# Row sums spread through DRAM, and half of a modulation vector summed on GpSimd, in a hybrid decoder block

## The chip, the cores and the metric

One core of one Trainium2 chip. The metric is the device time of one execution in microseconds (us), the median over runs; lower is better. Engines: TensorE (PE, with its weight loads as PEld), VectorE (DVE), ScalarE (ACT), GpSimd (POOL) and SyncE (SP), which here only issues DMAs.

## What is computed

One layer of a decoder trunk on x of 1024 tokens by 1024 channels, float32. A vector c gives shifts, scales and gates:

```python
c_act = jax.nn.silu(c)
mod = c_act @ w_mod[l] + b_mod[l]                      # 6 x 1024
h = _modulate(_rmsnorm(x, norm1_gain[l]), sh1, sc1)
x = x + g1 * _hybrid_mixer(h, ...)                     # attention and output projection
h = _modulate(_rmsnorm(x, norm2_gain[l]), sh2, sc2)
x = x + g2 * _swiglu(h, w_gate[l], w_up[l], w_down[l])
sh_f, sc_f = jnp.split(c_act @ w_mod_final + b_mod_final, 2, axis=-1)
return _modulate(_rmsnorm(x, final_gain), sh_f, sc_f)
```

The mixer has eight stick-breaking heads and eight sparse heads of 64. For a sparse head each query takes its 256 best keys by an indexer; then

```python
logits = q @ k_sel * scale - slopes * dist             # masked where not valid
p = jax.nn.softmax(logits, axis=-1)
out = p @ v_sel
```

Both groups are RMS-normalised, joined and multiplied by w_o (1024 x 1024).

## The kernel before, in words

The program is written out by hand, one instruction stream per engine, in two blocks with a barrier between them: phase 0 and 1 (modulation, norm, input projection, index selection) and the attention; then `phase4` (output projection and first residual) and `phase5` (FFN, final norm).

**Attention.** `attention` (L993) walks over 128 rows: 16 heads (8 stick-breaking, then 8 sparse), each with its eight 128-query blocks from the widest (i = 7, 1024 keys) to the narrowest (i = 0). Step r does the logits of row r + 2 on TensorE, row r on VectorE, and for the sparse half the exponential of row r - 1 on ScalarE (L1218), with its row sums into `sm`. Four rows are a group (`gr`, 32 in all; the upper group of a head has rows 7 to 4, the lower rows 3 to 0). A group's probabilities are transposed five steps later, block by block (L1469), copied from PSUM to `aT` by ScalarE (L1242) or VectorE (L1350), and multiplied with the values into the one PSUM bank `o` (L1487). The transposes' places are chosen by `attention_plan`: the bank `ps_at`, or the free half of a logits slot `ps_z`; for each it also says which earlier block must have been copied out.

A sparse group is divided by its row sums at the end. The sums stand one per partition (query), but `o` has the queries along its free dimension, so they have to be spread: VectorE takes the reciprocals of a group's 4 x 128 sums (L1354, step 4 d + 5 of the sparse half for group d); TensorE multiplies each column, broadcast, with an identity into a bank (L1494, step 4 d + 8; eight passes recorded for four matmuls); ScalarE copies 64 lanes of it to `spr` (L1249); VectorE multiplies `o` with it into `of` (L1365, step 4 d + 9), and that frees `o` for TensorE. SP loads `w_mod` tiles all through the attention, GpSimd sums them (L1278 product, L1282 sum).

**Output projection.** `phase4` (L1508) makes 16 half rows y(n) of 128 x 512. TensorE computes the stick-breaking part `y_sb` (L1678, three ahead) and the sparse part `y_d` (L1694), 12 matmuls each. ScalarE scales the first (L1627), VectorE adds the second (L1780, `y_full`), gates it (L1792) and adds it to x (L1795). Behind x of steps 0 to 7 VectorE does four of 32 steps of the final modulation vector: `fa` = `fa` + c_act[t] * w_mod_final tile (L1756 first of a quarter, L1759 the others). SP loads the tiles (L1593, four buffers) and stores `fa` after every quarter of eight steps (L1592, L1600); the next quarter waits for that store. ScalarE squares finished rows of x (L1617); after the fourth, GpSimd computes 1/rms of the first four rows (L1646, L1648, "early rstd"), VectorE scales them ahead of y step 8 (`early_xhat`, L2055), and TensorE transposes them between the later y steps (L2049); ScalarE modulates each transposed tile (L2015). SP stores every finished row of x (L2007) between its loads.

Of the kernel before, what the change touches and what calls it, by code (L numbers as in the profile page):

```python
# [25 lines left out]
P = 128  # L26
# [966 lines left out]
def attention(nc, k, g, A, scr, p1, base):  # L993
# [9 lines left out]
    def extra(r, end):  # L1003
        v = [("v", 2 * (r // (2 * NT)) + x) for x in range(2)] if values_at(r) else []
        return v, [("s", gr) for gr in range(SBG, 2 * SBG) if end.get(gr, -99) == r]
# [63 lines left out]
    sd = k.sem("rsum_spread_done")  # L1069
    sc = k.sem("rsum_spread_copied")  # L1070
# [28 lines left out]

    def spread(r):  # L1100
        return [gr for gr in end if gr >= SBG and end[gr] == r]
# [93 lines left out]
    def scalar(act):  # L1195
# [12 lines left out]
        for r in range(STEPS):  # L1208
# [4 lines left out]
            if SBR < r <= NR:  # L1213
# [5 lines left out]
                               accum_out=sm[:, c:c + 1]).then_inc(ex, 1)  # L1219
            if values_at(r):  # L1220
# [22 lines left out]
            for gr in spread(r):  # L1243
                d = gr - SBG
                lanes = slice(HD * (gr // 2 % 2), HD * (gr // 2 % 2) + HD)
                act.wait_ge(sd, d + 1)
                if d >= 4:
                    act.wait_ge(od, gr - 3)
                act.activation(spr[lanes, upper(gr)], place(("s", gr))[lanes], ACT.Copy).then_inc(sc, 1)  # L1249
# [60 lines left out]
    def vector(dve):  # L1310
        dve.wait_ge(cset, 1 + NPB)
        for r in range(STEPS):
# [42 lines left out]
            for gr in ended(r, 1):  # L1355
# [7 lines left out]
                else:  # L1363
                    dve.wait_ge(sc, gr - SBG + 1)
# [14 lines left out]
    def tensor(pe):  # L1379
        def await_freed(e):  # L1380
# [5 lines left out]
            elif kind == "s":  # L1386
                pe.wait_ge(sc, n - SBG + 1)
            else:
                pe.wait_ge(*copied(n))
# [59 lines left out]
        for r in range(STEPS):  # L1449
# [39 lines left out]
            for gr in spread(r):  # L1489
                d = gr - SBG  # L1490
                await_freed(follows["s", gr])
                pe.wait_ge(rc, d + 1)
                for b in range(4):
                    last = pe.matmul(place(("s", gr))[:, P * b:P * b + P],  # L1494
                                     rs[:, 4 * d + b:4 * d + b + 1].to_broadcast([P, P]), g.ident[:],
                                     start=True, stop=True)
                last.then_inc(sd, 1)
# [10 lines left out]
def phase4(nc, ctx, k, g, A, modf, then):  # L1508
# [14 lines left out]
    NFW = 4  # L1523
    fw = nc.alloc_sbuf_tensor_at("wmod_final", [P, NFW, HALF], F32, offset=g.top - 8 * 1024)
    ps_a, ps_b, ps_m = g.ps[:, 0:NSB], g.ps[:, NSB:NSB + ND4], g.ps[:, NSB + ND4]
# [26 lines left out]
    NF, FY = 4 * KD, 8  # L1552
# [24 lines left out]
    def sync(sp):  # L1577
# [16 lines left out]

        for n in range(NY):
            for f in final_steps(n):
                load_final(f)
# [1254 lines left out]
```

## Time and profile before

| what | us |
|---|---|
| median of 3 runs (1447.98 to 1451.27) | 1448.45 |
| the profiled execution | 1446.68 |
| its span in the profile | 1445.0 |
| TensorE busy | 1341.7 (93%) |
| VectorE busy | 1023.3 (71%) |
| GpSimd busy | 727.8 (50%) |
| ScalarE busy | 684.6 (47%) |

The span runs from the first to the last recorded instruction of the profiled execution; times within it are from its start. "Busy" leaves out waits, semaphore and DMA-issuing instructions. The chain of waits follows back from the last instruction what released each step. The sparse half of the attention lies at about 508 to 674 us, the output projection at 676 to 790 us.

### The profile page before, as it was taken

The numbers are of one execution on the slowest core, as the hardware profiler recorded it, in microseconds if no ns is written. First come the engines' busy times: TensorE is split into PE (matmuls) and PEld (weight loads), VectorE is DVE, ScalarE is ACT, GpSimd is POOL, SyncE is SP. The second block draws the span as 40 slices with busy tenths as digits, with TensorE's granted clock in tenths as the row PEclk, the third lists the DMA queues.
The fourth block names the chain that finished last, engine by engine and source line by source line (L and its number), as shares of the span: only waits on it lengthen the run. The fifth ranks groups of instructions, "written<-read, shape, count | busy, mean of one in ns | idle before, by whom it ended". The sixth has DMA issues, their size and how long they took to land.

```text
span 1445.0 us, 18548 instructions
## 1 busy us (share of the span) xinstructions
PE 1341.7 (93%) x6181; PEld 1071.6 (74%) x6181; DVE 1023.3 (71%) x1468; ACT 684.6 (47%) x1157; POOL 727.8 (50%) x628
## 2 busy tenths in 40 slices
PE   2899999997899999989998899999999999999997
PEld 2668888785566666657876778888888888887886
DVE  4678699987877655554775986666666666378787
ACT  5456677736676655554125633223323334354332
POOL 3135444556677866652002165555555556578552
PEclk9899899998999999998999999999999999999999
DMA  9521234457534343312753244444444435989432
GB/s 326 178 62 30 88 126 135 144 162 203 131 76 114 88 125 116 89 43 84 272 172 114 88 152 155 167 168 167 168 158 146 146 141 197 362 296 327 150 109 117
DMA packets 123562, 220.20 MB, mean 152 GB/s; under 512 B 9386, under 2 KB 52500, under 8 KB 123220
## 3 DMA queue, kind: packets, MB, share of 16 engines
q1 hardware_dynamic: 123476, 219.12, 45.7%
q8 instruction: 46, 0.75, 0.2%
q14 instruction: 40, 0.33, 0.1%
HBM read 160.90 MB, written 57.93 MB: 151 GB/s over the span
## 4 chain that ended last, share of the span: by engine, by line
PE 41%; DVE 7%; issue 2%; DMA 1%; ACT 1%; POOL 0%; DVEq 0%; POOLq 0%; ACTq 0%
PE ps_out L2339 25%; PE ps_out L2365 12%; PE ps_out L1694 1%; DVE mod_acc_final L1759 1%; PE ps_out L1678 1%; DMA scr_mod_final<-mod_acc_final 1%; DVE y_full L1780 1%; DVE wgu_lo L2446 0%; PE ps_out L1702 0%; ACT square_junk L2257 0%; DVE x L2601 0%; DVE y_gated L1792 0%; DVE down_part L2599 0%; DVE h_sum_t L2413 0%; DVE h_t_full L2413 0%
## 5 line engine op out<-in xcount | busy, mean ns | idle before, releaser
L2036 POOL TENSOR_TENSOR wgu_lo<-wgu_raw,wgu_hi 128x512 fp32r<-128x512 f32 x66 | 97.4, 1483 | 127.6 <-ACT wgu_hi L2028 127.6
L2273 POOL TENSOR_TENSOR dn_lo<-dn_raw,dn_hi 128x512 fp32r<-128x512 f32 x77 | 126.9, 1665 | 67.1 <-ACT dn_hi L2179 67.0
L2028 ACT ACTIVATE wgu_hi<-wgu_sum 128x512 fp32r<-128x512 f32 x88 | 55.2, 632 | 199.7 <-DVE wgu_sum L2429 80.0
L2339 PE MATMUL ps_out<-h_b_t_hi,wgu_hi 128*128 128x512 f32 x352 | 138.1, 392 | 6.6 <-DVE h_b_t_lo L2417 2.6
L483 POOL TENSOR_TENSOR win_lo<-win_raw,win_hi 128x256 fp32r<-128x256 f32 (+1 forms) x84 | 66.7, 824 | 141.0 <-ACT win_hi L473 115.7
L2339 PE MATMUL ps_out<-h_b_t_hi,wgu_lo 128*128 128x512 f32 x352 | 137.7, 391 | 0.0
L2339 PE MATMUL ps_out<-h_b_t_lo,wgu_hi 128*128 128x512 f32 x352 | 137.5, 391 | 0.0
L2179 ACT ACTIVATE dn_hi<-dn_raw 128x1024 fp32r<-128x1024 f32 x77 | 81.2, 1062 | 114.4 <-PE ps_out L2365 55.7
L2365 PE MATMUL ps_out<-dn_hi 128*128 128x512 f32 x308 | 120.2, 390 | 0.0
L2365 PE MATMUL ps_out<-dn_hi,dn_lo 128*128 128x512 f32 x308 | 119.8, 389 | 0.0
L2365 PE MATMUL ps_out<-dn_lo,dn_hi 128*128 128x512 f32 x308 | 119.8, 389 | 0.0
L2497 DVE TENSOR_TENSOR dn_lo<-dn_raw,dn_hi 128x512 fp32r<-128x512 f32 x77 | 84.7, 1132 | 44.6 <-ACT dn_hi L2179 44.6
L1292 POOL TENSOR_TENSOR a_rows<-beta,stick_left 128x1024 f32<-128x1024 f32 (+3 forms) x64 | 83.7, 1314 | 49.0 <-DVE stick_left L1319 28.6
L839 DVE TENSOR_SCALAR_CACHE_REDUCE cmp_junk<-score,thr 128x768 uint8<-128x768 f32 (+3 forms) x96 | 103.8, 1131 | 1.3 <-DVE thr L863 0.2
L2036 POOL TENSOR_TENSOR wgu_lo<-wgu_sum,wgu_hi 128x512 fp32r<-128x512 f32 x40 | 60.7, 1519 | 76.3 <-ACT wgu_hi L2028 76.3
L1319 DVE TENSOR_TENSOR_SCAN stick_left<-ps_z,scan_zero 128x1024 f32<-128x1024 f32 (+3 forms) x64 | 85.5, 1345 | 12.2 <-ACT ps_z L1205 8.2
L107 PE MATMUL ps_proj<-hTh,win_hi 128*128 128x512 f32 (+1 forms) x288 | 90.1, 394 | 2.6 <-ACT proj_full L593 1.6
L107 PE MATMUL ps_proj<-hTl,win_hi 128*128 128x512 f32 (+1 forms) x288 | 89.7, 393 | 0.0
L107 PE MATMUL ps_proj<-hTh,win_lo 128*128 128x512 f32 (+1 forms) x288 | 89.4, 392 | 0.0
L631 ACT ACTIVATE cmp_junk<-score,thr 128x384 int8<-128x384 f32 (+2 forms) x93 | 66.0, 711 | 36.3 <-DVE thr L863 36.2
L2339 PEld LDWEIGHTS ps_out<-h_b_t_hi,wgu_hi 128*128 128x128 f32 x352 | 66.5, 189 | 21.4 <-issue 5.2
L1487 PE MATMUL ps_o<-aT,vd 128*128 128x512 f32 (+1 forms) x192 | 73.8, 493 | 4.1 <-DVE o_full L1365 2.9
(356 smaller groups left out, 3648.9 us busy)
## 6 DMA issues: line engine op xcount, KB each, us to landing
scr_act_sums<-act_sums SPq DMA_DIRECT2D x11, 1792.0 KB, 6.7
dn_raw<-scr_act_sums SPq DMA_DIRECT2D x77, 256.0 KB, 5.3
wmod_c<-in_w_mod_dram SPq DMA_DIRECT2D x48, 256.0 KB, 2.9
wgu_raw<-in_w_gate_dram SPq DMA_DIRECT2D x11, 1024.0 KB, 5.3
wgu_raw<-in_w_up_dram SPq DMA_DIRECT2D x11, 1024.0 KB, 5.4
wd_sums<-in_w_down_dram SPq DMA_DIRECT2D x11, 1024.0 KB, 4.8
scr_wd_sums<-wd_sums SPq DMA_DIRECT2D x11, 1024.0 KB, 4.1
dn_raw<-scr_wd_sums SPq DMA_DIRECT2D x44, 256.0 KB, 7.0
```

The source lines that it names most:

```text
L107: last = pe.matmul(ps[:, s], w[:, t, :], x[:, t, s], start=(t == 0 and w is wh and x is xh), stop=(t == KD - 1 and w is wl))
L483: last = pool.tensor_tensor(low[:, t:t + 2, 0:w], raw[:, n % 2, t:t + 2, 0:w], high[:, t:t + 2, 0:w].bitcast(F32), ALU.subtract)
L839: last = dve.tensor_scalar(junk[:, w], g.score[:, w], at(i - 2), None, op, ALU.add, accum_out=cnt[:, i - 2:i - 1])
L1292: pool.tensor_tensor(a[gr % 2][:, rows[r][1] % 4, 0:w], bt[:, r % NB, 0:w], pb[:, r % NPB, SEQ - w + 1:SEQ + 1], ALU.mult).then_inc(mul, 1)
L1319: dve.tensor_tensor_scan(pb[:, r % NPB, SEQ - w:SEQ][:, ::-1], z[:, r % NZ, 0:w][:, ::-1], zero[:].to_broadcast([P, w]), 1.0, ALU.mult, AL ...
L1487: pe.matmul(o[:, s], v, aT[:, n % NA, s], start=(b == 0), stop=(b == 4 * upper(gr) + 3), skip_group_check=True).then_inc(vd, 1)
L2036: pool.tensor_tensor(sl[slot(m, x)][:], src, sh[slot(m, x)][:].bitcast(F32), ALU.subtract).then_inc(wlp, 1)
L2179: act.activation(bh[q % NSLOT][:], braw[entry(q)][:], ACT.Copy).then_inc(dhi, 1)
L2273: pool.tensor_tensor(bl[q % NSLOT][:, 1], braw[entry(q)][:, 1], bh[q % NSLOT][:, 1].bitcast(F32), ALU.subtract).then_inc(dlw, 1)
L2339: last = pe.matmul(bank(m, b), a[s][:, t], h[x][t // 2][:, t % 2], start=(fresh and t == 0 and a is sh and h is hh), stop=(t == 3 and a is ...
L2365: last = pe.matmul(ps[:, y], a[s][:, 0, P * b:P * b + P], w[s][:, 1], start=(fresh and q % NPR == 0 and a is bh and w is bh), stop=(q % NP ...
L2497: dve.tensor_tensor(bl[q % NSLOT][:, 0], braw[entry(q)][:, 0], bh[q % NSLOT][:, 0].bitcast(F32), ALU.subtract).then_inc(dla, 1)
```

## The change

Part one: a sparse group's reciprocals are no longer spread by TensorE and ScalarE. ScalarE stores the 512 floats to a DRAM row (step 4 d + 6), waits for that store at step 4 d + 7, and loads the row back, broadcast to the 64 lanes of `spr`. VectorE waits for the load where it waited for the copy. The planner has no place to find for the spread any more.

Part two: of the final modulation vector VectorE sums the first two quarters, GpSimd the last two, each in a tile of its own (`fa`, `fb`) with two load buffers (`fw`, `fx`) instead of four. GpSimd does them after `rstd_col` and ahead of the early rstd. SP issues for each f first the GpSimd load, then the VectorE load.

```diff
@@ attention
-        return v, [("s", gr) for gr in range(SBG, 2 * SBG) if end.get(gr, -99) == r]
+        return v, []
@@ attention, scalar, behind the exponential of step r
+            d = (r - SBR - 6) // 4
+            if r >= SBR + 6 and r % 4 == 2 and d < SBG:
+                act.wait_ge(rc, d + 1)
+                act.dma_start(rsum[d].rearrange("(b p) -> p b", p=P), rs[:, 4 * d:4 * d + 4],
+                              allow_slow_non_contiguous=True).then_inc(rso, 16)
@@ attention, scalar, behind the copies to aT
-            for gr in spread(r):
-                d = gr - SBG
-                lanes = slice(HD * (gr // 2 % 2), HD * (gr // 2 % 2) + HD)
-                act.wait_ge(sd, d + 1)
+            d = (r - SBR - 7) // 4
+            if r >= SBR + 7 and r % 4 == 3 and d < SBG:
+                lanes = slice(HD * (d // 2 % 2), HD * (d // 2 % 2) + HD)
+                act.wait_ge(rso, 16 * (d + 1))
                 if d >= 4:
-                    act.wait_ge(od, gr - 3)
-                act.activation(spr[lanes, upper(gr)], place(("s", gr))[lanes], ACT.Copy).then_inc(sc, 1)
+                    act.wait_ge(od, SBG + d - 3)
+                act.dma_start(spr[lanes, upper(d)], rsum[d:d + 1, :].partition_broadcast(HD)).then_inc(rsl[d % 2], 16)
@@ attention, vector
-                    dve.wait_ge(sc, gr - SBG + 1)
+                    dve.wait_ge(rsl[gr % 2], 16 * ((gr - SBG) // 2 + 1))
                     dve.tensor_tensor(of[lanes, G], o[lanes], spr[lanes, G], ALU.mult).then_inc(od, 1)
@@ attention, tensor
-            for gr in spread(r):
-                d = gr - SBG
-                await_freed(follows["s", gr])
-                pe.wait_ge(rc, d + 1)
-                for b in range(4):
-                    last = pe.matmul(place(("s", gr))[:, P * b:P * b + P],
-                                     rs[:, 4 * d + b:4 * d + b + 1].to_broadcast([P, P]), g.ident[:],
-                                     start=True, stop=True)
-                last.then_inc(sd, 1)
@@ phase4
-    NFW = 4
+    fb = nc.alloc_sbuf_tensor_at("mod_acc_final_pool", [P, HALF], F32, offset=g.top - 14 * 1024)
+    NFW = 2
     fw = nc.alloc_sbuf_tensor_at("wmod_final", [P, NFW, HALF], F32, offset=g.top - 8 * 1024)
+    fx = nc.alloc_sbuf_tensor_at("wmod_final_pool", [P, NFW, HALF], F32, offset=g.top - 4 * 1024)
-    NF, FY = 4 * KD, 8
+    NF, FY = 2 * KD, 8
@@ phase4, sync
+        def load_final_pool(f):
+            c, t = f // KD, f % KD
+            if f >= NFW:
+                sp.wait_ge(fpa, f - NFW + 1)
+            if f >= KD and t == NFW - 1:
+                sp.dma_start(modf[:, half(2 + c - 1)], fb[:]).then_inc(fpo, 16)
+            sp.dma_start(fx[:, f % NFW], A["w_mod_final"][P * t:P * t + P, half(2 + c)]).then_inc(fxl[f % NFW], 16)
+
         for n in range(NY):
             for f in final_steps(n):
+                load_final_pool(f)
                 load_final(f)
             if n == FY:
                 sp.wait_ge(fmd, NF)
-                sp.dma_start(modf[:, half(3)], fa[:]).then_inc(fmo, 16)
+                sp.dma_start(modf[:, half(1)], fa[:]).then_inc(fmo, 16)
+                sp.wait_ge(fpa, NF)
+                sp.dma_start(modf[:, half(3)], fb[:]).then_inc(fpo, 16)
@@ phase4, gpsimd, behind rstd_col and ahead of the early rstd
+        for f in range(NF):
+            c, t = f // KD, f % KD
+            pool.wait_ge(fxl[f % NFW], 16 * (f // NFW + 1))
+            by = g.csil[:, t:t + 1].to_broadcast([P, HALF])
+            if t == 0:
+                if c:
+                    pool.wait_ge(fpo, 16 * c)
+                pool.tensor_tensor(fb[:], fx[:, f % NFW], by, ALU.mult).then_inc(fpa, 1)
+            else:
+                pool.tensor_tensor(fx[:, f % NFW], fx[:, f % NFW], by, ALU.mult).then_inc(fpr, 1)
+                pool.wait_ge(fpa, f)
+                pool.wait_ge(fpr, f - c)
+                pool.tensor_tensor(fb[:], fb[:], fx[:, f % NFW], ALU.add).then_inc(fpa, 1)
         pool.wait_ge(s2, 4)
@@ phase5, scalar and sync: wherever all of fmo (fmd) is awaited
-            act.wait_ge(p4.fmo, 64)
+            act.wait_ge(p4.fmo, 32)
+            act.wait_ge(p4.fpo, 32)
```

## Rows read from the trace of the kernel before

**Rows 1.** The page, busy time: us, share of the span, instructions.

```profile
PE 1341.7 (93%) x6181; PEld 1071.6 (74%) x6181; DVE 1023.3 (71%) x1468; ACT 684.6 (47%) x1157; POOL 727.8 (50%) x628
```

**Rows 2.** Stretch of one sparse head: length, busy by engine, clock, DMA.

```profile
598.80:619.00 20.20, 18.86 (x102) 13.57 (x101) 10.62 (x29) 10.97 (x26) 15.08 (x14) 1.00 0.39 110
```

**Rows 3.** Timeline, TensorE, projection: start, us, what [idle before, and releaser].

```profile
752.90 0.66 PE L2049 MATMUL ps_out<-ident,x 128*128 128x128 f32 x4 [0.72 <-DVE x L2055]
...
759.56 1.09 PE L2049 MATMUL ps_out<-ident,x 128*128 128x128 f32 x4 [3.24 <-ACT h_sum_b L2015]
```

**Rows 4.** The tile scr_mod_final, all its DMAs: time to landing.

```profile
DMA to landing us min/median/max: 2.4/4.6/5.0
```

**Rows 5.** Timelines of VectorE, GpSimd and SP in the projection.

```profile
750.12 2.73 DVE L2055 TENSOR_SCALAR x<-x,rstd 128x1024 f32<-128x1024 f32 x4
...
748.60 1.01 POOL L1648 TENSOR_TENSOR rstd<-rstd,nhalf 128x4 f32<-128x4 f32 x1
...
706.79 0.33 SPq L2007 DMA_DIRECT2D scr_x<-x  x1
```

**Rows 6.** Timeline, TensorE, around both spreads of one head.

```profile
599.46 1.05 PE L1494 MATMUL ps_at<-ident,prob_rsum 128*128 128x128 f32 x8
601.20 0.66 PE L1469 MATMUL ps_at<-ident,a_rows 128*128 128x128 f32 x4 [0.68 <-ACT rsum_spread L1249]
...
607.00 1.05 PE L1494 MATMUL ps_at<-ident,prob_rsum 128*128 128x128 f32 x8
607.89 1.04 PE L1469 MATMUL ps_z<-ident,a_rows 128*128 128x128 f32 x8
```

**Rows 7.** Timeline, VectorE: widest row of the first two sparse heads.

```profile
498.46 1.28 DVE L1334 CUSTOM_DVE_ANT_0 a_rows<-ps_z,score,nslope 128x1024 f32<-128x1024 f32 x1 [3.13 <-PE ps_at L1469]
...
516.22 1.28 DVE L1334 CUSTOM_DVE_ANT_0 a_rows<-ps_z,score,nslope 128x1024 f32<-128x1024 f32 x1 [3.11 <-PE ps_at L1469]
```

**Rows 8.** Timelines of VectorE and ScalarE in that head of rows 6.

```profile
597.55 1.28 DVE L1334 CUSTOM_DVE_ANT_0 a_rows<-ps_z,score,nslope 128x1024 f32<-128x1024 f32 x1 [3.11 <-PE ps_at L1469]
...
598.96 1.14 DVE L1334 CUSTOM_DVE_ANT_0 a_rows<-ps_z,score,nslope 128x896 f32<-128x896 f32 x1
...
602.70 1.03 ACT L1218 ACTIVATE a_rows<-a_rows,neg_max 128x896 f32<-128x896 f32 x1
...
603.84 1.00 DVE L1334 CUSTOM_DVE_ANT_0 a_rows<-ps_z,score,nslope 128x768 f32<-128x768 f32 x1
...
605.82 0.81 ACT L1218 ACTIVATE a_rows<-a_rows,neg_max 128x640 f32<-128x640 f32 x1
...
609.66 0.65 DVE L1365 TENSOR_TENSOR o_full<-ps_o,rsum_spread 64x512 f32<-64x512 f32 x1
```

**Rows 9.** DMA: issues with count, KB each, median us to landing; queue's packets.

```profile
q1 hardware_dynamic: 123476, 219.12, 45.7%
...
wmod_c<-in_w_mod_dram SPq DMA_DIRECT2D x48, 256.0 KB, 2.9
...
wmod_final<-in_w_mod_final_dram SPq DMA_DIRECT2D x32, 256.0 KB, 4.0
...
scr_x<-x SPq DMA_DIRECT2D x8, 512.0 KB, 2.8
...
wukv_raw<-in_w_uk_dram SPq DMA_DIRECT2D x1, 64.0 KB, 2.0
```

**Rows 10.** Stretch at the projection's first steps; last numbers: DMA share, GB/s.

```profile
696.00:699.00 3.00, 3.00 (x14) 2.46 (x14) 0.15 (x1) 0.00 (x0) 0.00 (x0) 1.00 1.03 390
```

**Rows 11.** GpSimd's product and sum in the attention: ns min/median/max, first, last start.

```profile
L1278 POOL TENSOR_TENSOR mod_prod_c<-wmod_c,csil x42: 1032/1041/3022, 362.6 to 649.1; 128x512 f32<-128x512 f32 x42
...
L1282 POOL TENSOR_TENSOR mod_acc_late<-mod_acc_late,mod_prod_c x28: 1261/1276/1291, 525.8 to 650.2; 128x512 f32<-128x512 f32 x28
```

**Rows 12.** Timeline, GpSimd and VectorE, where both read two SBUF tiles.

```profile
838.07 1.62 POOL L2265 TENSOR_TENSOR wd_sums<-wd_sums 128x512 f32<-128x512 f32 x1
...
846.94 1.77 DVE L2486 TENSOR_TENSOR act_sums<-act_sums 128x512 f32<-128x512 f32 x1
```

More of the change, by code:

```diff
@@ L990, in attention_plan, with attention @@
     return rows, units, of_step, end, done_by, bank, follows, row_follows
-def attention(nc, k, g, A, scr, p1, base):
+def attention(nc, k, g, A, scr, rsum, p1, base):
     NZ, LEAD, VSTEP = 3, 5, 3
@@ L1068, in attention @@
     rc = k.sem("d_rsum_ready")
-    sd = k.sem("rsum_spread_done")
-    sc = k.sem("rsum_spread_copied")
+    rso = k.sem("rsum_stored")
+    rsl = k.sems("rsum_spread_loaded", 2)
     oll = k.sem("oT_lo_last_ready")
@@ L1098, in ended @@
         return [gr for gr in end if end[gr] + steps == r]
-    def spread(r):
-        return [gr for gr in end if gr >= SBG and end[gr] == r]
     def paired(r, steps):
@@ L1385, in await_freed @@
                 pe.wait_ge(v_rdy, n + 1)
-            elif kind == "s":
-                pe.wait_ge(sc, n - SBG + 1)
             else:
@@ L1551, in phase4 @@
     fmo = k.sem("mod_final_stored")
-    NF, FY = 4 * KD, 8
+    fxl = k.sems("wmod_final_pool_loaded", NFW)
+    fpr = k.sem("mod_final_pool_product")
+    fpa = k.sem("mod_final_pool_added")
+    fpo = k.sem("mod_final_pool_stored")
+    NF, FY = 2 * KD, 8
     STEP_T = {(1, 10): 0, (0, 10): 1, (1, 11): 2, (0, 11): 3, (1, 12): 4, (0, 12): 5, (1, 13): 6, (0, 13): 7}
@@ L1802, in phase4 @@
     p.yam, p.yfr, p.ysc, p.x1r, p.s2, p.rs2, p.fmd, p.fmo, p.ybm = yam, yfr, ysc, x1r, s2, rs2, fmd, fmo, ybm
+    p.fpa, p.fpo = fpa, fpo
     p.NY, p.NF = NY, NF
@@ L2139, in sync @@
                 sp.wait_ge(u2n, 4)
-                sp.wait_ge(p4.fmo, 64)
+                sp.wait_ge(p4.fmo, 32)
+                sp.wait_ge(p4.fpo, 32)
                 sp.dma_start(mfin[:], modf.rearrange("p (c n) -> p c n", c=4)).then_inc(mfl, 16)
@@ L2181, in scalar @@
         act.wait_ge(p4.fmd, p4.NF)
+        act.wait_ge(p4.fpa, p4.NF)
         copy_p1(0)
@@ L2700, in emit @@
         scr = nc.dram_tensor("scr_qkv", [16, 2, P, SEQ], F32, kind="Internal").ap()
+        rsum = nc.dram_tensor("scr_rsum", [2 * NH, HALF], F32, kind="Internal").ap()
         modf = nc.dram_tensor("scr_mod_final", [P, 2 * D], F32, kind="Internal").ap()
@@ L2759, in emit @@
                 assert base + 68 * 1024 <= nc.sbuf_top
-                pa = attention(nc, k, g, A, scr, p1, base)
+                pa = attention(nc, k, g, A, scr, rsum, p1, base)
                 with nc.Block() as block:
```

## The prediction

> **What bounds the kernel now.** I read the page's busy shares first, then the chain of waits, then the two stretches that the diff touches: the sparse half of the attention (508 to 674 us) and the output projection (676 to 790 us). TensorE is busy 93% of the span [rows 1]. In the sparse half one head takes 20.2 us; TensorE works 18.9 of them, VectorE and ScalarE 11, GpSimd up to 15 [rows 2]: TensorE goes through its instructions nearly without a gap. So it does in the projection, up to the first transposes of the normed rows at 752.90, where it waits 0.72 us, and the next at 759.56, where it waits 3.24 us [rows 3]. VectorE is the late one there. The chain of waits has it three times at the store of a finished quarter of the final modulation vector, which lands in 4.6 us at the median [rows 4], and the scaling of x that the transposes read (L2055) starts only at 750.12 [rows 5].
>
> **Part one: the spread leaves TensorE.** Each of the 16 groups loses eight TensorE passes (L1494) and one ScalarE copy (L1249). For a lower group the passes begin at 607.00 and what follows begins at 607.89: 0.89 us. For an upper group it is 599.46 to 601.20, 1.74 us, since the next transposes also wait for ScalarE's copy out of the same bank, 0.68 us [rows 6]. That wait is there in seven of the eight heads. That makes 1.74 + 0.89 = 2.63 us a head. The trace has a check on it: the first sparse head runs while no spread is due yet, and from its widest row to the next head's it takes 516.22 - 498.46 = 17.8 us [rows 7] instead of 20.2 [rows 2], 2.4 less. I take the 2.4, which has the waits in it that come in the spread's place: 7 x 2.4 = 16.8 us, and the last head 2 x 0.89 = 1.8: gross 18.6 us. The planner now places the transposes of steps 5 and 6 otherwise: a block then waits for ScalarE's copy of one step before, which comes earlier too, without the spread's copy in front of it. I take 0 for that.
>
> What is added is on ScalarE's queue: at step 2 or 6 of a head's eight a store of 512 single floats, at step 3 or 7 a wait for its landing, then the broadcast load. Behind the wait stand the exponentials of the next rows, and TensorE's transposes wait for the fourth of them. Take the lower group in the head at 597 us, with rows named by their key block. VectorE ends row 7 at 598.83 and row 6 at 600.1; the spread's copy no longer holds ScalarE, so row 6's exponential (1.03) runs from 600.1, or from 600.5 in every second head, where a square stands between: the store goes out at 601.1 or 601.5. VectorE's row 5 ends at 603.1 (604.84 moved 1.74 up), its exponential near 604.05, being a little longer than row 4's 0.81. Then the load's issue, 0.35 as on SP [rows 5], and row 4 with the gap behind it, 0.9: done at 605.3. TensorE now wants it at 607.89 - 2.63 = 605.26 [rows 6, 8]. So a store that has landed costs nothing. The cover is 605.26 - 0.9 - 0.35 - 601.1 (or 601.5) = 2.9 (or 2.5) us of landing, and each us beyond costs 1 us a head.
>
> How long does such a store take? The trace has none. A 512 KB store lands in 2.8 us, a 64 KB load in 2.0, a 256 KB load in 2.9 [rows 9]. 512 KB at the 390 GB/s of a full stretch [rows 10] are 1.3 us, so 1.5 are fixed: the lower end. For the upper end let each float cost what a mean packet costs: 45.7% of 16 engines' 1445 us over 123476 packets is 86 ns, and 32 of them per engine 2.7 us, on top of the 2.4 us of the shortest store in the projection: 5.1 [rows 4, 9]. I take 2.7 us, nearest to the 512 KB store: a piece of 4 bytes should cost less than a packet with data. The loss is then 0 or 0.2 us a head, with some row-4 jitter 1.5 us in all. At 1.5 us there is none, at 5.1 it is 8 x 2.4 = 19.2 us. The upper groups have more cover: behind their store and one more exponential ScalarE waits for TensorE's transposes anyway (its copy of 613.7), and then come exponentials that nobody wants before the next head. The load's 128 KB should lie between the 64 and the 256 KB, 2.4 us, and land 5.5 us after the store's issue, at 606.8 or so; VectorE's product wants it at 609.66 - 2.63 = 607.0 [rows 8]. That is even, and behind it on VectorE stand only rows of which TensorE wants none for 1 us.
>
> Each group also has two more waits for a DMA, and a released wait lets a little pass before the next instruction starts: 16 times some 0.07 us, 1.1 us, my allowance and not a row. Part one: -18.6 + 1.5 + 1.1 = -16 us.
>
> The Trainium skill, DMA: Bandwidth & Descriptors, "Rules for kernel authors", says that a strided last dimension becomes one descriptor per element, and its section "Anatomy of one DMA" gives about 2 us of fixed cost per transfer, most of it the receipt of the write. It speaks against this edit. By its 2 us the store would be within the cover; no row here shows the cost of one such element.
>
> **Part two: half of the final vector to GpSimd.** VectorE loses 16 steps and two of three waits for a store. But what holds TensorE is the start of the scaling at 750.12, and that also waits for GpSimd's early rstd, ready at 749.61 [rows 5]. In the new code GpSimd comes to this rstd only after its 16 steps. So the question is when the sixteenth ends.
>
> A step on GpSimd is a product, 1.04 us, and a sum, 1.28, alone [rows 11]. It will not be alone. Where VectorE and GpSimd both read two SBUF tiles, a VectorE instruction of 0.69 us takes 1.77 and GpSimd's sum takes 1.62, one pair each 1.7 us [rows 12]; VectorE has four such in every y step. I take 3.3 us a step. A load takes 2.9 to 4.0 us [rows 9]; I take 3.3, for one or two are in flight and not five. A buffer's load is issued when its last reader is done, so with two buffers two steps cost one landing and one step, 6.6 us. The first loads sit behind the x rows, which fill the DMA engines until 699 [rows 10]; the second step ends at about 701. Seven pairs more: 46.2 us. SP's queue adds to it: the third and fourth GpSimd load stand behind loads that wait for VectorE's first steps, and the fifth behind the first x1 store (706.79) [rows 5], 2 us; the ninth step waits for the store of a half (4.6 instead of 3.3), 1.3 us. Sum: 750.5. Then rstd, 1.4 us, and a gap: the scaling starts at 752.1 instead of 750.12. The transposes and the chain behind them (y steps 8 and 9 on VectorE, square, ScalarE's modulation) move with it: +2.0 us. VectorE itself keeps up: 0.8 + 4 x 1.6 = 7.2 us in a step at worst beside TensorE's 5.45, which puts y step 7 near 746. SP's wait for the sixteenth step holds back only x1 stores that aren't ready, ScalarE's new waits are long over.
>
> The ends: if the two engines did not slow each other, a step costs 2.4 and a pair 5.7, the sixteenth ends 6.3 us earlier, and both waits of TensorE (0.72 and 3.24) [rows 3] go: -4 us. If every load takes 4.0, seven pairs cost 5 us more, less what the waits on SP then hide: +6 us.
>
> **Sum.** -16 + 2 = -14 us. The profiled execution took 1446.68 us, 1.68 more than its span; the median of the runs is 1448.45. So 1432.7 there, and 1434.5 at the median.
>
> **Rivals.**
> (a) GpSimd's instructions keep their 1.04 and 1.28 us. For it: VectorE will idle in part. Against: the long instructions of [rows 12]. Part two is then -4 instead of +2: -20, 1428.5.
> (b) GpSimd is far behind, by loads of 4.0 us or longer blocking: part two +6, sum -10, 1438.5. The Trainium skill, SBUF — State Buffer, "SBUF: two separate sides", calls the shared port an exclusive lock, the loser fully blocked. By that a pair would cost 0.69 + 1.28 = 1.97 us; the trace's 1.7 has them overlap a little, so this case stays the weaker one.
> (c) The store lands at 4.0 to 4.5 us: 1.3 to 1.8 us a head, 10 to 14 us and not 1.5; total -5 to -1: 1445. For it: 512 pieces beside SP's weight loads on the same DMA engines. Against: nothing queues in front of it.
> (d) Slower than before: ScalarE's wait for the store decides. Its place is step 3 of each sparse head, its price 8 us per us of landing, and what the sum leaves is eaten at 2.7 + 15.5 / 8 = 4.6 us. At 5.9 us: 8 x 3.2 = 25.6 and not 1.5, so +10: 1458.5.
> (e) The spread's passes only filled time in which TensorE would wait anyway for another engine's rows: part one gives nothing, the kernel is at +2 to +4, 1451. Against it: the first head's 17.8 us [rows 7], and that no other engine has more than 15 of 20.2 us [rows 2].
>
> **How the numbers follow.** Main case 0.52, (a) 0.12, (b) 0.14, (c) 0.14, (d) and (e) 0.08 together. The range 1427 to 1446 holds the first three and the better half of (c). A measurement of this kernel can't tell a change under 0.3%, 4.3 us, from none: faster 0.84, same 0.08, slower 0.08.
>
> **What would show it.** A sparse head of about 18.0 us, with no L1494 and no wait of L1469 for a spread. The store's landing near 2.7 us. TensorE waiting at L1469 for ScalarE's a_rows by less than 0.5 us a head. In the projection GpSimd busy from 697 to 750.5 (all 16 us earlier by then), its instructions 1.2 to 1.7 us long; L2055 right behind rstd L1648; the wait of the first transposes (L2049) grown from 0.72 to near 3 us. I am wrong if the store's landing is over 3.5 us, if heads stay at 20 us, or if GpSimd's last step ends before VectorE's.

## The result, and the profile after

| | before | after |
|---|---|---|
| median of 4 runs each, us | 1449.10 (1447.98 to 1451.27) | 1518.32 (1513.26 to 1526.00) |
| ratio, 95% interval | | 1.0493 (1.0470 to 1.0517) |
| profiled execution / its span, us | 1446.68 / 1445.0 | 1515.03 / 1513.3 |
| mean granted clock of TensorE | 0.977 | 0.952 |
| widest row of the first to that of the last sparse head, us | 144.05 | 192.20 |

The kernel is 4.9% slower where a gain of 14 us was forecast. Span and busy time of the changed kernel, from its page:

```profile
PE 1350.9 (89%) x6053; PEld 1076.4 (71%) x6053; DVE 1030.3 (68%) x1452; ACT 678.6 (45%) x1141; POOL 766.7 (51%) x658
```

TensorE has 128 instructions fewer than in [rows 1] and still is busy for 9 us more. Both have one cause, and one sparse head shows it. Stretches of the changed kernel, in the columns of [rows 2]: the whole head, and 4 us pieces of it.

```profile
603.72:631.78 28.06, 19.51 (x86) 14.02 (x85) 10.96 (x26) 10.88 (x25) 10.96 (x10) 0.88 0.44 70
```
```profile
604.00:608.00 4.00, 4.00 (x24) 3.00 (x22) 3.43 (x8) 2.44 (x5) 3.42 (x4) 1.00 0.41 111
608.00:612.00 4.00, 3.56 (x15) 1.80 (x13) 3.37 (x9) 1.46 (x3) 3.55 (x4) 1.00 0.54 114
612.00:616.00 4.00, 0.00 (x0) 0.00 (x0) 0.40 (x2) 0.00 (x0) 0.11 (x1) 1.00 0.02 6
616.00:620.00 4.00, 2.42 (x12) 2.46 (x13) 0.45 (x1) 2.98 (x8) 0.00 (x0) 0.54 0.26 33
620.00:624.00 4.00, 4.00 (x16) 3.44 (x16) 2.47 (x8) 2.12 (x5) 1.54 (x2) 0.61 1.12 162
```

From 612 to 616 everything stands, the DMA engines included (share 0.02). What it stands for is in ScalarE's timeline, and in TensorE's behind it: the store goes out at 607.08, the load that waits for it at 616.01.

```profile
607.08 0.37 ACTq L1220 DMA_DIRECT2D scr_rsum<-prob_rsum  x1
...
616.01 0.45 ACTq L1251 DMA_DIRECT2D rsum_spread<-scr_rsum  x1
616.51 0.83 ACT L1215 ACTIVATE a_rows<-a_rows,neg_max 128x640 f32<-128x640 f32 x1 [6.08 <-DMA scr_rsum<-prob_rsum]
...
629.98 0.63 ACT L1256 ACTIVATE o_dT_hi<-o_full 128x512 fp32r<-128x512 f32 x1 [3.66 <-DMA scr_rsum<-prob_rsum]
```
```profile
617.58 1.09 PE L1469 MATMUL ps_at<-ident,a_rows 128*128 128x128 f32 x4 [5.93 <-ACT a_rows L1215]
...
631.32 0.33 PE L1469 MATMUL ps_at<-ident,a_rows 128*128 128x128 f32 x1 [2.54 <-ACT aT L1244]
```

The exponential of row 4 (640 keys) starts 6.08 us late and TensorE's transposes 5.93 us late; the upper group's store holds ScalarE once more for 3.66 us, and through ScalarE's copy TensorE for 2.54 us. After the first stop the granted clock is 0.54 and 0.61 in the next two pieces, so nearly at the lower of its two levels (1.2 of 2.4 GHz), where the kernel before stays at 1.00 through such a head [rows 2]. The head's 28.06 us are 19.51 busy and 8.55 idle.

The same from the widest row of the first sparse head to the start of the projection block, before and changed:

```profile
498.46:676.50 178.04, 160.69 (x842) 114.16 (x840) 94.78 (x221) 94.60 (x218) 98.14 (x84) 1.00 0.27 80
```
```profile
498.77:736.60 237.83, 167.72 (x714) 117.07 (x712) 96.12 (x221) 88.52 (x202) 98.52 (x84) 0.88 0.42 69
```

Of the 59.8 us that the stretch is longer, TensorE idles for 52.8 (70.1 against 17.4) and works for 7.0 (167.7 against 160.7), although its 128 passes of the spread are gone.

The waits of the whole stretch 490 to 760 (engine, tile and line; releaser; us in total, times, longest), and how long the stores and the loads took (us to landing, minimum, median, maximum):

```profile
ACT a_rows L1215 <- DMA scr_rsum<-prob_rsum: 61.9, 12, 6.7
...
PE ps_at L1469 <- ACT a_rows L1215: 42.4, 8, 6.6
POOL mod_prod_c L1280 <- DMA wmod_c<-in_w_mod_dram: 42.2, 12, 7.9
...
PE ps_at L1469 <- ACT aT L1244: 16.6, 8, 4.1
```
```profile
L1220 ACTq DMA_DIRECT2D scr_rsum<-prob_rsum x16: 361/367/423, 508.7 to 719.6; - x16
DMA to landing us min/median/max: 7.7/9.0/9.7
```
```profile
L1251 ACTq DMA_DIRECT2D rsum_spread<-scr_rsum x16: 452/452/503, 518.4 to 727.4; - x16
DMA to landing us min/median/max: 3.2/4.1/7.6
```
```profile
wmod_c<-in_w_mod_dram SPq DMA_DIRECT2D x48, 256.0 KB, 7.0
```

A store of 2 KB takes 9.0 us, nearly twice the upper end that I had given it (5.1), and SP's loads of the attention's modulation weights land in 7.0 us instead of 2.9 [rows 9].

In the projection the first transposes of the normed rows wait 7.45 us where they waited 0.72 [rows 3]. VectorE, GpSimd and TensorE of the changed kernel there:

```profile
815.12 1.82 DVE L1780 SCALAR_TENSOR_TENSOR mod_acc_final<-wmod_final,csil,mod_acc_final 128x512 f32<-128x512 f32 x1 [2.82 <-DMA wmod_final<-in_w_mod_final_dram]
818.13 2.74 DVE L2078 TENSOR_SCALAR x<-x,rstd 128x1024 f32<-128x1024 f32 x4 [1.19 <-POOL rstd L1669]
```
```profile
815.13 1.26 POOL L1665 TENSOR_TENSOR mod_acc_final_pool<-mod_acc_final_pool,wmod_final_pool 128x512 f32<-128x512 f32 x1
816.48 0.52 POOL L1667 TENSOR_SCALAR rstd<-ss 128x4 f32<-128x4 f32 x1
817.08 1.02 POOL L1669 TENSOR_TENSOR rstd<-rstd,nhalf 128x4 f32<-128x4 f32 x1
```
```profile
820.92 1.12 PE L2072 MATMUL ps_out<-ident,x 128*128 128x128 f32 x4 [7.45 <-DVE x L2078]
```

The projection block begins at 736.6 and not at 676.5, so 60.1 of the 68.3 us of span are lost before it. Its last y_full starts at 855.01 instead of 787.32, 67.7 us later: another 7.6 us in the block, and next to nothing behind it. (The expectations of part1, part2 and both_16b work with 61.4 and 6.3 us, from a start read as 737.9.)

### The profile page after: what moved, and what is told of

It reads as the page before. It is cut to its first block, busy times and chain, and to the rows that moved or that the text cites. A ratio compares the mean times of both kernels' runs of the same rounds, so it can differ in the third digit from the quotient of the medians.

```text
span 1513.3 us, 18305 instructions
## 1 busy us (share of the span) xinstructions
PE 1350.9 (89%) x6053; PEld 1076.4 (71%) x6053; DVE 1030.3 (68%) x1452; ACT 678.6 (45%) x1141; POOL 766.7 (51%) x658
## 4 chain that ended last, share of the span: by engine, by line
PE 40%; DVE 5%; issue 2%; POOL 2%; DMA 1%; ACT 1%; SPq 0%; DVEq 0%; POOLq 0%; ACTq 0%
PE ps_out L2364 25%; PE ps_out L2390 12%; PE ps_out L1715 1%; DMA wmod_final_pool<-in_w_mod_final_dram 1%; PE ps_out L1699 1%; POOL mod_acc_final_pool L1665 1%; POOL wmod_final_pool L1662 0%; PE ps_out L1723 0%; DVE x L1816 0%; DVE y_full L1801 0%; ACT square_junk L2282 0%; DVE y_gated L1813 0%; DVE x L2626 0%; DVE down_part L2624 0%; DVE wgu_lo L2471 0%
## 5 line engine op out<-in xcount | busy, mean ns | idle before, releaser
L1469 PE MATMUL ps_at<-ident,a_rows 128*128 128x128 f32 x282 | 54.3, 309 | 65.4 <-ACT a_rows L1215 42.4
L1469 PEld LDWEIGHTS ps_at<-ident,a_rows 128*128 128x128 f32 x282 | 39.6, 159 | 88.7 <-issue 61.7
L1215 ACT ACTIVATE a_rows<-a_rows,neg_max 128x1024 f32<-128x1024 f32 (+3 forms) x64 | 49.3, 771 | 86.4 <-DMA scr_rsum<-prob_rsum 61.9
```

Of the source, the lines that this page charges most:

```text
L1469: last = pe.transpose(place(("u", n))[:, P * q:P * q + P], a[gr % 2][:, q, P * b:P * b + P], g.ident[:])
```

## The experiments

Twelve kernels, in four groups; each group ran on one chip with its own runs of the kernel before, and each ratio is against those.

| kernel | time, us | ratio to before, 95% | landing of the store, us |
|---|---|---|---|
| part1 | 1529.56 | 1.0539 (1.0507 to 1.0572) | 9.9 |
| part2 | 1451.58 | 1.0012 (0.9999 to 1.0025) | none |
| p1_sp | 1519.42 | 1.0480 (1.0456 to 1.0504) | 9.5 |
| p1_nowait | 1477.40 | 1.0204 (1.0163 to 1.0244) | 9.6 |
| p1_nostore | 1427.97 | 0.9852 (0.9831 to 0.9872) | none |
| probe | 1447.85 | 1.0003 (0.9988 to 1.0019) | three shapes |
| p1_16b | 1426.79 | 0.9860 (0.9835 to 0.9885) | 2.9 |
| both_16b | 1432.53 | 0.9899 (0.9881 to 0.9916) | 2.7 |
| both_early | 1436.01 | 0.9916 (0.9898 to 0.9935) | 3.0 |
| probe2 | 1448.19 (one run) | | three shapes |
| both_idle | 1424.82 | 0.9826 (0.9799 to 0.9853) | 3.0 |
| both_light | 1430.07 | 0.9870 (0.9847 to 0.9893) | 3.0 |

### Which part, and who waits

**part1** has only the hunks of the attention, **part2** only those of the output projection.

> The first part alone: sparse sums through DRAM, the final modulation vector left whole on VectorE as before. Theory (the store decides): ScalarE stands before its load until the store has landed, which in the changed kernel took 9.0 us, so sparse heads take 27 to 31 us here too, and the kernel 1512 us (1518.3 less the 6.3 that the projection block lost). Rival (the two parts hurt each other, or the loss sits in GpSimd's part): under 1470 us.

> The second part alone: half of the final modulation vector on GpSimd, the sparse sums spread on TensorE as before. Theory: the projection block is longer by the 6.3 us that it was in the changed kernel, because GpSimd's sixteenth step ends only then and the scaling of x waits for it: 1449.1 + 6.3 = 1455.4 us. Rival (that loss came over from the slow start, from transfers or clock of the attention block): 1449 to 1451 us, the sixteenth step 74 us after the block's start instead of 78.5.

The first part alone is 5.4% slower, the second 0.1%. So all of the large loss is the first part's. part1 is 18 us above the 1512 that I expected and 11 us slower than both parts together; its store took 9.9 us and not 9.0, but it ran on another chip, so I read nothing into that. For the second part the first theory's 1455.4 was too much: 1449.19 became 1451.58, +2.4 us. Its trace still has TensorE waiting 5.1 us for the scaling of x, which starts 77.9 us after the block's start where it was 73.6 before.

**p1_sp** moves wait and load to SyncE:

```
             # ScalarE, step 3 or 7 of a head
-            act.wait_ge(rso, 16 * (d + 1))
...
-            act.dma_start(spr[lanes, upper(d)], rsum[d:d + 1, :].partition_broadcast(HD)).then_inc(rsl[d % 2], 16)
             # SyncE, ahead of its next load of modulation weights
+            sp.wait_ge(rso[d % 4], 16 * (d // 4 + 1))
...
+            sp.dma_start(spr[lanes, upper(d)], rsum[d:d + 1, :].partition_broadcast(HD)).then_inc(rsl[d % 2], 16)
```

> The first part alone, with the wait for the store and the load issued by SyncE instead of ScalarE, ahead of the next weight load of its queue. Theory (what costs is that ScalarE stands in that wait with exponentials and copies queued behind it): the store still takes about 9 us, ScalarE's 61.9 us of waiting are gone, and the kernel comes to 1440 to 1465 us, the rest being VectorE's wait for the later load. Rival (the store itself slows the other transfers and the clock, whoever waits): it stays at 1495 to 1515 us.

ScalarE's waits were gone, and the time stayed, 1519.42: my theory fell, and the rival's 1495 to 1515 was a little low. Where the wait went is in the answer for VectorE's product (who it waited for, and who waited for it; us, times):

```profile
  DMA rsum_spread<-scr_rsum: 83.3, 11
  PE ps_o L1499: 2.3, 4
who waited for it (us, times):
  PE ps_o L1499: 68.0, 11
```

Store and load one after the other are 9.5 + 5.3 = 14.8 us at the medians, longer than a half head of 9 to 10 us. TensorE needs ps_o back within that, whichever engine stands in the wait. So this run moved the wait and did not take it away; it doesn't decide between theory and rival.

**p1_nowait** keeps stores and loads, but the load reads rows of the final modulation weights and needs no store. **p1_nostore** leaves out the store too.

```
-            act.wait_ge(rso, 16 * (d + 1))
...
-            act.dma_start(spr[lanes, upper(d)], rsum[d:d + 1, :].partition_broadcast(HD)).then_inc(rsl[d % 2], 16)
+            act.dma_start(spr[lanes, upper(d)], A["w_mod_final"][d:d + 1, 0:HALF].partition_broadcast(HD)).then_inc(rsl[d % 2], 16)
```

> The first part alone, but the load reads rows of the final modulation weights instead of the stored sums, so nothing waits for the store; the same stores and loads are made, and the values that scale the sparse heads are wrong. Theory (the wait decides): granted clock of the sparse heads back at 1.00, heads at 17.8 to 20.2 us, kernel 1430 to 1440 us, though the store still takes 9 us. Rival (interference of the 512 small pieces with the other transfers): modc weight loads still land late, kernel over 1480 us.

> The first part alone without any store of the sums; the load reads rows of the final modulation weights, so the values that scale the sparse heads are wrong. Against the kernel that keeps the stores but waits for none (1477 us) it shows what the stores cost by being in the queues. Theory (512 pieces hold up the load behind them and SyncE's weight loads): the load lands in 2 to 4 us, heads at 17.8 to 20.2 us, 1430 to 1436 us. Rival (16 spread loads of 128 KB are themselves too much for queues and buffers): modulation weights still land 5 us or later and the kernel stays over 1450 us.

DMA issues of the two, 490 to 760 us (KB each, median us to landing), first p1_nowait, then p1_nostore:

```profile
wmod_c<-in_w_mod_dram SPq DMA_DIRECT2D x37, 256.0 KB, 8.0
...
rsum_spread<-in_w_mod_final_dram ACTq DMA_DIRECT2D x16, 128.0 KB, 8.5
...
scr_rsum<-prob_rsum ACTq DMA_DIRECT2D x16, 2.0 KB, 9.6
```
```profile
wmod_c<-in_w_mod_dram SPq DMA_DIRECT2D x37, 256.0 KB, 2.9
...
rsum_spread<-in_w_mod_final_dram ACTq DMA_DIRECT2D x16, 128.0 KB, 3.0
```

Neither theory was right about p1_nowait: it lay between them, at 1477, and its heads behind the first take 21.5 to 26.1 us. Taking the wait away gives back 1529.6 - 1477.4 = 52 us, taking the store away another 1477.4 - 1428.0 = 49 us (across two chips; by the ratios 51). In p1_nowait nothing waits for the store. But a load issued behind it takes 8.5 us instead of 3.0, and SyncE's loads, on another queue, 8.0 instead of 2.9: while the slow store is under way, other transfers are late. Which of them costs time is in the waits of p1_nowait:

```profile
DVE o_full L1367 <- DMA rsum_spread<-in_w_mod_final_dram: 40.4, 13, 6.7
...
PE ps_o L1487 <- DVE o_full L1367: 33.4, 13, 5.7
```

VectorE's product waits for the load behind the store, and TensorE for the product. SyncE's late loads hold GpSimd (66.9 us, 20 times), and no wait of TensorE in the attention leads back to them. In part1 and the changed kernel the load is issued only when the store has landed, so the 52 and the 49 us are the same slow store met in two ways, not two costs of the changed kernel side by side.

### What makes the store slow

> The kernel before, with ScalarE issuing a store of the four columns of reciprocals once per half head, which nothing waits for until the block's end, in three shapes in turn: 512 pieces of 4 bytes side by side in DRAM (six times), 128 pieces of 16 bytes (five), 512 pieces of 4 bytes each 64 bytes from the next (five). Theory (a store costs by its pieces): 9 to 10 us, 3.5 to 4 us, 9 to 10 us. Rival (it costs because neighbouring 4-byte writes hit the same 64 bytes of DRAM): the spaced one lands in under 5 us. Time 1449 plus what the transfers behind the stores lose: up to 16 x 1.5 us, to 1473 us, if they are delayed as in the changed kernel, 1449 to 1452 if the modulation loads have that much slack.

> The kernel before with unwaited stores, as in the first probe, in three further shapes: 512 pieces of 4 bytes each 8 bytes from the next (8 share 64 bytes of DRAM), each 16 bytes from the next (4 share them), and one column alone, 128 pieces of 4 bytes side by side (16 share them). Theory (writes into the same 64 bytes go one after the other, about 0.5 us each: 16 of them 8.9 us, at most 4 of them 2.3 to 2.6): 4.5 us, 2.6 us, and 8 to 9 us for the one column although it has a quarter of the pieces. Rival (each 4-byte piece that has neighbours costs by itself, 512 of them 8.9 us): 8.9, 8.9 or 2.6, and 3 to 4 us for the one column.

Both probes are the kernel before plus one store per half head that nothing waits for, in shapes taken in turn. In the first the time is that of the kernel before: its 9 us stores were one in three and nobody was waiting. The edit of the first (the second changes the target's pattern, and for the one column the source):

```
+                act.wait_ge(rc, d + 1)
+                src = rs[:, 4 * d:4 * d + 4]
+                x = d % 3
+                dst = (lambda: prb[0][d].rearrange("(b p) -> p b", p=P),
+                       lambda: prb[1][d].rearrange("(p b) -> p b", p=P),
+                       lambda: prb[2][d].rearrange("(b p) x -> p b x", p=P)[:, :, 0])[x]()
+                act.dma_start(dst, src, allow_slow_non_contiguous=True).then_inc(prd[x], 16)
```

The answers for three of the shapes, one tile each: prb_4b and prb_4b_lines of the first probe, prb_4b_one_column of the second.

```profile
L1229 ACTq DMA_DIRECT2D prb_4b<-prob_rsum x6: 366/367/423, 506.6 to 662.6; - x6
...
DMA to landing us min/median/max: 8.2/8.9/11.8
```
```profile
L1229 ACTq DMA_DIRECT2D prb_4b_lines<-prob_rsum x5: 366/366/417, 526.7 to 653.5; - x5
...
DMA to landing us min/median/max: 1.9/2.6/3.9
```
```profile
L1229 ACTq DMA_DIRECT2D prb_4b_one_column<-prob_rsum x5: 338/338/353, 529.4 to 655.6; - x5
...
DMA to landing us min/median/max: 7.4/7.9/9.2
```

All six shapes:

| shape | pieces that share 64 bytes of DRAM | landing, us: median (lowest to highest), count |
|---|---|---|
| 512 x 4 B, side by side | 16 | 8.9 (8.2 to 11.8), 6 |
| 128 x 4 B, side by side (one column) | 16 | 7.9 (7.4 to 9.2), 5 |
| 512 x 4 B, every 8 B | 8 | 5.3 (3.1 to 7.8), 6 |
| 512 x 4 B, every 16 B | 4 | 3.0 (2.5 to 4.7), 5 |
| 128 x 16 B, side by side | 4 | 2.3 (1.4 to 9.5), 5 |
| 512 x 4 B, every 64 B | 1 | 2.6 (1.9 to 3.9), 5 |

The wide range of the 16 byte shape goes with what was ahead of it: its five landings are 1.4, 1.4, 2.3, 7.0 and 9.5 us, and the last two are those of the stores issued at 546.9 and 608.0, while the 4 byte store before them (539.7 and 600.9, landing after 8.2 and 11.8 us) was still under way. Before the other three it had landed.

My theory of the first probe fell: the same 512 pieces of 4 bytes land in 2.6 us when each has 64 bytes to itself. The number of pieces hardly matters, for a quarter of them, side by side, still takes 7.9 us. The time goes with how close together the pieces lie: counted by blocks of 64 bytes, one piece in a block lands in 2.6 us, and up to sixteen add about 0.4 us each ((5.3 - 2.6) / 7, (8.9 - 2.6) / 15), those with four a little less. That they are done one after the other in a block is a reading that fits the six shapes; the trace shows landings only. The 64 is the spacing that I tried, and these six shapes don't fix the size of the block. With blocks of 16 bytes the counts are 4, 4, 2, 1, 1, 1 in the table's order, with blocks of 512 they are 128, 128, 64, 32, 32, 8, and both put the shapes in about the same order. A block of 8 bytes doesn't fit, for with it a piece every 8 bytes would be as fast as one every 64.

The Trainium skill, DMA: Bandwidth & Descriptors, "Specifications", says that below 512 bytes the DMA engine reads, modifies and writes. It gives no price. All six shapes have pieces below that size, so this alone doesn't tell them apart; the runs show three of them at 2.3 to 3.0 us, and slow ones only where 4 byte pieces lie side by side or every 8 bytes.

### The repair

**p1_16b** is part1 with the four values of a partition stored side by side, 16 bytes at a time; VectorE reads the spread row with a stride to undo that.

```
-            act.dma_start(rsum[d].rearrange("(b p) -> p b", p=P), rs[:, 4 * d:4 * d + 4],
+            act.dma_start(rsum[d].rearrange("(p b) -> p b", p=P), rs[:, 4 * d:4 * d + 4],
...
-            dve.tensor_tensor(of[lanes, G], o[lanes], spr[lanes, G], ALU.mult).then_inc(od, 1)
+            dve.tensor_tensor(of[lanes, G].rearrange("q (b p) -> q b p", p=P),
+                              o[lanes].rearrange("q (b p) -> q b p", p=P),
+                              spr[lanes, G].rearrange("q (p b) -> q b p", p=P), ALU.mult).then_inc(od, 1)
```

> The first part alone, its store in 128 pieces of 16 bytes (the four sums of a partition side by side) and VectorE's product reading the spread row with a stride of 16 bytes to undo that order; the output is the reference's. Theory (the cost is the number of pieces, each at about 7.5 us / 512): store 3.5 to 4 us, ScalarE's wait under 1.5 us a half head, kernel 1440 to 1450 us. Rival (the landing of a small DRAM store is what it is): store 7 us or more and kernel over 1480 us.

1426.79 us, better than both theories: 103 us less than part1 (across two chips; by the ratios 98) by the order in which the values lie in DRAM. Its store's landing, and one of its heads:

```profile
L1220 ACTq DMA_DIRECT2D scr_rsum<-prob_rsum x16: 321/327/368, 509.1 to 646.8; - x16
DMA to landing us min/median/max: 1.4/2.9/6.4
```
```profile
571.87:589.97 18.10, 16.97 (x86) 11.59 (x85) 11.63 (x26) 10.84 (x25) 11.21 (x11) 1.00 0.38 103
```

The head takes 18.1 us with the clock at 1.00. VectorE's strided product takes 1.07 us where it took 0.69, and nobody waits for it beyond 4.6 us in all (TensorE, eight times).

### The second part on a sound first part

**both_16b** is the changed kernel with that one edit. **both_early** also moves GpSimd's early rstd:

```
         for f in range(NF):
+            if f == NF - 2:
+                pool.wait_ge(s2, 4)
+                pool.tensor_scalar(g.rstd2[:, 0:4], g.ss2[:, 0:4], 1.0 / D, EPS, ALU.mult, ALU.add).then_inc(v2, 1)
+                pool.wait_ge(v2, 1)
+                pool.tensor_tensor(g.rstd2[:, 0:4], g.rstd2[:, 0:4], g.nhalf[:, 0:4], ALU.pow).then_inc(rs2, 1)
...
```

> The changed kernel with one edit: the store in 128 pieces of 16 bytes, VectorE's product undoing the order with a stride. Both parts stand as changed. Theory (all of the loss hangs on the shape of the store, and the second part costs the 2.4 us that it cost alone): 1426.8 + 2.4 = 1429 us. Rival (the 6.3 us that the projection block lost in the changed kernel belong to the second part whenever the first is there): 1433 us.

> The kernel both_16b with one move: GpSimd computes the first four root mean squares before its last two steps of the final modulation vector and not behind the sixteenth. Theory (the second part loses because the scaling of x, and TensorE's transposes behind it, wait for GpSimd's sixteenth step, which with the root ended 6 us later than before): the roots come 5 us earlier, TensorE's wait for x goes, 3 to 5 us faster than both_16b: 1424 to 1426 us. Rival (the loss is GpSimd's and VectorE's shared port): no change, or slower by the 0 to 3 us that late steps hold back the last store.

both_16b came to 1432.53 us, where the rival stood. Against p1_16b, ratio to ratio, the second part costs 0.0039 x 1448 = 5.6 us, but that compares two chips, and the two intervals leave it anything from 1 to 10. Moving the root gained nothing, 1436.01. VectorE of both_early and TensorE:

```profile
737.68 1.30 DVE L1783 SCALAR_TENSOR_TENSOR mod_acc_final<-wmod_final,csil,mod_acc_final 128x512 f32<-128x512 f32 x1 [3.24 <-DMA wmod_final<-in_w_mod_final_dram]
739.00 4.43 DVE L2081 TENSOR_SCALAR x<-x,rstd 128x1024 f32<-128x1024 f32 x4
```
```profile
743.48 1.12 PE L2075 MATMUL ps_out<-ident,x 128*128 128x128 f32 x4 [7.64 <-DVE x L2081]
```

The scaling did start earlier, by 1.2 us within the block, and then took 4.43 us instead of 2.73 [rows 5] while GpSimd's last two steps ran beside it; and ahead of it VectorE's own last step stood for its load, 3.24 us. So moving the root alone is not enough. Two more kernels separate GpSimd's work from its loads:

```
 both_idle:  product and sum of GpSimd's 14 later steps on columns 0:8 instead of 0:512
 both_light: its loads from the third on read 64 of the 512 columns
```

> The kernel both_16b (1432.5 us), with GpSimd's product and sum of 14 of its 16 steps cut to 8 of the 512 columns: the same loads, waits and order, nearly no work on GpSimd's side of the port (half of the final modulation vector comes out wrong). Theory (the 5.7 us that the second part adds come from the shared port: VectorE's steps at 1.4 to 1.8 us where they took 0.75): 1424 to 1427 us, VectorE's steps back at 0.75 us. Rival (they come from loads that land too late for two buffers, one VectorE step waiting 2.8 us right ahead of the scaling of x): 1430 to 1433 us with VectorE's steps short.

> The kernel both_16b with GpSimd's loads from the third on cut to 64 of 512 columns, so 32 KB instead of 256 KB each, while GpSimd works on all 512 columns as before (half of the final modulation vector comes out wrong). Theory (the port): VectorE's steps stay at 1.4 to 1.8 us and the time at 1431 to 1434 us. Rival (the loads): VectorE's loads land sooner, its waits for them (5.2 us) and GpSimd's (11 us) go, and the kernel comes to 1425 to 1428 us.

VectorE's steps (ns minimum, median, maximum), in both_16b, both_idle and both_light in this order:

```profile
L1782 DVE SCALAR_TENSOR_TENSOR mod_acc_final<-wmod_final,csil,mod_acc_final x14: 969/1528/1822, 689.8 to 739.6; 128x512 f32<-128x512 f32 x14
```
```profile
L1783 DVE SCALAR_TENSOR_TENSOR mod_acc_final<-wmod_final,csil,mod_acc_final x14: 745/752/755, 686.1 to 729.3; 128x512 f32<-128x512 f32 x14
```
```profile
L1783 DVE SCALAR_TENSOR_TENSOR mod_acc_final<-wmod_final,csil,mod_acc_final x14: 753/1528/1819, 684.2 to 729.7; 128x512 f32<-128x512 f32 x14
```

With GpSimd's work away the ratio falls by 0.0073 (10.6 us), VectorE's steps are back at 0.75 us, and TensorE's transposes don't wait for the scaling although VectorE still waits 9.1 us for its loads. With the loads cut it falls by 0.0029 (4.2 us, as wide as its interval) and the steps stay at 1.5 us. TensorE's wait for the scaling, in both_16b and both_light:

```profile
PE ps_out L2074 <- DVE x L2080: 7.1, 1, 7.1
```
```profile
PE ps_out L2075 <- DVE x L2081: 2.5, 1, 2.5
```

| kernel | scaling starts after the block's start, us | TensorE waits for it, us |
|---|---|---|
| p1_16b | 73.1 | 0.3 |
| both_16b | 80.0 | 7.1 |
| both_early | 78.8 | 7.6 |
| both_light | 75.4 | 2.5 |
| both_idle | 70.3 | 0 |

These are single profiles, and the block itself differs by 3 us with the granted clock (p1_nostore, with p1_16b's block, has 76.1). So GpSimd's work weighs more, but cutting the loads takes most of TensorE's wait away too. And both_idle takes away two things at once: what GpSimd's work does to VectorE's steps, and the length of GpSimd's own steps, for its sixteenth ends 68.7 us after the block's start instead of 78.3. How much of the loss is the one and how much the other isn't shown.

## Why the prediction was wrong

**The step that failed is the landing of the store**: "I take 2.7 us, nearest to the 512 KB store: a piece of 4 bytes should cost less than a packet with data", with 5.1 as the upper end. It was 9.0. Both ends came from counting bytes and packets, and neither asks where the pieces land. [rows 9] has no transfer that writes small neighbouring pieces, so no row there could bound this; the upper end should have been open. The paragraph that the prediction set aside (one descriptor for each float) pointed at the right transfer, though the count of pieces turned out not to be what costs; and the fixed cost of about 2 us in it is near what the store takes in pieces of 16 bytes (2.3 and 2.9 us).

**Rival (d)** had the place right (step 3 of a head, ScalarE's exponential of row 4, TensorE's transposes behind it). With 9.0 us its price gives 8 x (9.0 - 2.9) = 49 us of wait. The head shown has it nearly to the tenth: 6.1 forecast, 6.08 and 5.93 read at 616.51 and 617.58. Over all eight heads TensorE waits 42.4 us there. But -14 - 1.5 + 49 = +33 us, and +69 were measured. That sum left out three things:
- the upper group, called covered, holds TensorE too: 2.54 us in the head shown, 16.6 us in all eight, where the kernel before has 3.8;
- after a stop TensorE works at the lower clock for a while: its instructions of the head take 19.51 us, and 16.97 in p1_16b. The 28.06 - 18.10 = 9.96 us between these heads are 7.42 of idle (8.55 against 1.13) and 2.54 of longer instructions. Over the whole stretch I estimate the clock at 21 us: 7.0 us more work, and 16 x 0.89 = 14 us of passes that are gone [rows 6];
- the projection block lost 7.6 us and not 2.

With 42.4 in the place of 49, and with 12.8, 21 and 5.6 us for these three, +33 becomes +66.

"Nothing queues in front of it", against rival (c), looked at the wrong side: what is issued beside or behind such a store is late (p1_nowait). In the changed kernel SP's modulation loads are, at 7.0 us, but no wait of TensorE leads back to them.

**The gross gain was right.** "A sparse head of about 18.0 us" is 18.0 to 18.1 in most heads of p1_16b (one takes 18.9), and the first part, forecast at -16 us (18.6 less small deductions), measured -20 (-24 to -17 by the ratio's interval). There the store of 2.9 us stays in its cover of 2.9 us, and p1_nostore, which has no store to wait for, is no faster beyond the intervals. The allowances of 1.5 and 1.1 us are not to be seen. Rival (e), gaps filled anyway, is refuted by p1_16b.

**Part two** was forecast at +2 and measured +2.4 alone (-0.1 to +3.6); in the changed kernel's profile the block lost 7.6, and about 5.6 on p1_16b. Rival (b), at +6, described that better. That +2.4 came so near may be luck, for in part2's trace too the scaling starts 4.3 us later within the block, and not 2. From the end of its second step to that of its sixteenth GpSimd took 53.0 us in the changed kernel (763.4 to 816.4), where 49.5 were added up. Its steps were shorter than the 3.3 us taken (product and sum 1.15 and 1.55 us at the median), its loads slower, 3.9 us at the median against 3.3: the term for the load was the one too small. "VectorE itself keeps up" was wrong: its last step waits 2.82 us for its load and then takes 1.82 instead of 0.75, and the scaling of x, which gates TensorE, stands behind it on the same engine. both_early fits that: with the root out of the way the time stayed lost.

Rival (a), no slowing between the two engines, is refuted by GpSimd's sums (1.55 us at the median and not 1.28) and by VectorE's steps in both_16b and both_idle (1.53 and 0.75 us). Its price of -4 is what an unhindered part two may be worth: both_idle, with nearly no work on GpSimd, is 4.9 us faster than p1_16b by the ratios, though the two intervals don't tell that from none.

The best version with the right output is p1_16b, 1.4% faster than the kernel before (1.1 to 1.7), with the second part left out.

## What to carry to other kernels

Before a small result goes through DRAM, look at the order of its pieces there: values of one partition side by side, so that the pieces have 16 bytes and not 4, and let a strided read undo the order. Where a transfer of a kind that the trace lacks lies on the path, measure it alone in a copy of the kernel, with nothing waiting for it, before building on it. Work moved from VectorE to GpSimd isn't gone when both read two tiles from SBUF: add what each slows the other and how soon its load buffers come round, and look at which instruction of VectorE stands right behind the last shared one.

## What the runs showed of the hardware

- 128 floats stored side by side by 128 partitions land in 7.9 us, 512 floats spaced by 64 bytes in 2.6 us, and by 16 bytes in 3.0 us.
- While stores of 2 KB that take 9.6 us are under way, transfers of another queue are late (256 KB loads 8.0 us in p1_nowait, 2.9 in p1_nostore), and the DMA share of such a stretch need not show it: 0.02 from 612 to 616 us in the changed kernel, though 0.49, with 16 GB/s moved, in a like stop of part1 (600 to 604).
- TensorE's granted clock fell to 0.54 after it had stood for about 6 us, and was back at 1.00 in the piece that starts at 624, some 6 us after it had started again.
- VectorE's 512 column step with two SBUF operands beside GpSimd takes 1.53 us at the median and 0.75 with GpSimd idle; the four-instruction scaling of 1024 columns 4.43 us instead of 2.74.
